# The skipped general path of two expert stages, moved ahead of the last scatter

## The reference

```python
def hier_moe(h, wg, bg, we, be, w_gate, w_up, w_down):
    t = h.reshape(-1, d)                                  # 256 tokens
    ...                                                   # top group of 4, then the best 2 of its 4 experts
    comb = ((g_oh * gw)[:, :, None] * w_grp[:, None, :]).reshape(n, MOE_EXPERTS)
    a = jax.nn.silu(jnp.einsum('td,edf->tef', t, w_gate)) * jnp.einsum('td,edf->tef', t, w_up)
    y = jnp.einsum('tef,efd->td', a * comb[:, :, None].astype(a.dtype), w_down)

x = x + g2 * hier_moe(h, ...)        # g2 is the gate; then comes the next layer's norm of x
```

## Time and profile before

| | us |
|---|---|
| median of 3 runs | 1435.12 |
| lowest and highest | 1433.93, 1435.15 |
| the profiled execution, its own time | 1437.19 |
| its span in the trace | 1435.4 |
| TensorE busy with matmuls | 1319.3 (92%) |
| VectorE busy | 446.6 (31%) |
| ScalarE busy | 237.7 (17%) |

### The profile page before, as it was taken

One profiled execution on the slowest core, in us unless ns is written; L12 is line 12 of the kernel. 1 busy time (PEld: TensorE's weight loads), 2 busy tenths in 40 slices (PEclk: granted clock), 3 DMA queues, 4 the chain that ended last, 5 costly groups with the idle time before them and its releaser, 6 DMA issues.

```text
span 1435.4 us, 18899 instructions
## 1 busy us (share of the span) xinstructions
PE 1319.3 (92%) x7788; PEld 682.9 (48%) x7788; DVE 446.6 (31%) x1251; ACT 237.7 (17%) x589; POOL 104.3 (7%) x196
## 2 busy tenths in 40 slices
PE   4999988999899899889998999989999699999996
PEld 3446644443545665444435864554545333333232
DVE  2004552221313574522215452351132711201113
ACT  0003310111101453101111221111320211010000
POOL 1100000000011000000001000000000021322111
PEclk8999999999999799999999999999999799999998
DMA  9957936999953664369998442364336579999990
GB/s 357 370 148 265 329 118 224 366 340 348 335 194 130 216 233 141 132 218 367 340 347 321 165 158 92 120 251 171 120 115 227 184 267 352 363 386 387 386 346 31
DMA packets 214763, 357.43 MB, mean 249 GB/s; under 512 B 15845, under 2 KB 86038, under 8 KB 214678
## 3 DMA queue, kind: packets, MB, share of 16 engines
q1 hardware_dynamic: 200864, 352.33, 69.1%
q10 hardware_dynamic: 13814, 3.87, 1.2%
HBM read 355.14 MB, written 1.05 MB: 248 GB/s over the span
## 4 chain that ended last, share of the span: by engine, by line
PE 83%; DVE 7%; DMA 4%; ACT 3%; issue 2%; SPq 0%; POOL 0%; DVEq 0%; ACTq 0%
PE bank L2055 19%; PE bank L2236 8%; PE bank L2433 7%; PE bank L2262 4%; PE bank L2277 4%; PE bank L2294 4%; PE bank L2723 4%; PE bank L2148 4%; PE bank L2507 3%; PE bank L2073 3%; PE bank L2772 3%; DMA ring<-in_w_down 3%; PE bank L2400 2%; PE bank L2542 2%; PE bank L2140 1%
## 5 line engine op out<-in xcount | busy, mean ns | idle before, releaser
L2055 PE MATMUL bank<-ring,hT 128*128 128x512 f32 x416 | 182.3, 597 | 2.6 <-ACT hT L878 2.4
L2055 PEld LDWEIGHTS bank<-ring,hT 128*128 128x128 f32 x416 | 78.7, 192 | 97.6 <-issue 97.6
L2236 PE MATMUL bank<-ring,A 128*64 128x512 f32 x512 | 113.4, 595 | 6.2 <-issue 3.2
L2055 PE MATMUL bank<-ring,OT 128*128 128x512 f32 x224 | 97.2, 593 | 1.3 <-ACT OT L1167 0.8
L2073 PE MATMUL bank<-ring,cact 128*32 128x128 f32 x2304 | 80.8, 295 | 13.7 <-DMA ring<-in_ada_w 7.5
L2433 PE MATMUL bank<-ring,A 128*64 128x512 f32 x384 | 86.8, 597 | 0.0
L746 POOL TENSOR_TENSOR rstd<-rstd,nhalf 128x1 f32<-128x1 f32 x20 | 17.2, 860 | 896.5 <-DVE rstd L1233 896.5
L2073 PEld LDWEIGHTS bank<-ring,cact 128*32 128x32 f32 x2304 | 67.8, 119 | 29.1 <-issue 21.5
L2262 PE MATMUL bank<-pb 128*128 128x128 f32 (+1 forms) x512 | 64.4, 279 | 7.7 <-DVE A L1451 5.4
L2236 PEld LDWEIGHTS bank<-ring,A 128*64 128x64 f32 x512 | 36.2, 137 | 72.0 <-issue 68.7
L2262 PEld LDWEIGHTS bank<-pb 128*128 128x128 f32 x512 | 59.6, 192 | 20.1 <-issue 11.4
(11 more groups left out here) (439 smaller groups left out, 1611.8 us busy)
## 6 DMA issues: line engine op xcount, KB each, us to landing
ring<-in_ada_w SPq DMA_DIRECT2D x24, 2048.0 KB, 9.3
ring<-in_moe_w_gate SPq DMA_DIRECT2D x32, 1024.0 KB, 8.0
ring<-in_moe_w_up SPq DMA_DIRECT2D x32, 1024.0 KB, 10.5
ring<-in_moe_w_down SPq DMA_DIRECT2D x16, 2048.0 KB, 12.8
ring<-in_w_gate SPq DMA_DIRECT2D x16, 2048.0 KB, 10.3
ring<-in_w_up SPq DMA_DIRECT2D x16, 2048.0 KB, 10.8
ring<-in_w_down SPq DMA_DIRECT2D x16, 2048.0 KB, 19.9
ring<-in_w_in SPq DMA_DIRECT2D x13, 2048.0 KB, 12.8
```

The lines of the kernel that those rows point to most:

```text
L2055: ins = mm(B[2 * (m % 2) + tt][:], lhs[:, c, tt * P:(tt + 1) * P], w[:, c, :], start=c == 0, stop=c == C - 1)
L2236: ins = mm(B[4][n * b:n * (b + 1), :], h3[:, c, n * b:n * (b + 1)], wv[b][:, :, c, :], start=c == 0, stop=c == C - 1)
```

## The change

In the first two expert stages the branch around the general path comes before the last scatter on TensorE, and before the wait for the summed banks on VectorE. So that a body that does run can add into the same banks, it no longer opens and closes them: `start` and `stop` follow `large`, which is true in "moe2" alone. Its spread weights go to B[4] to B[7], for which two waits are added inside the body, and VectorE's adds at the end of the body are left to the adds of the main path. The memset that counts `moe_added` stands behind those adds. In "moe2" the place is the same, and only the memset is gone.

```diff
@@ ScalarE, moe_rest_act
-                    a.copy(combT[:, 2 * j:2 * j + 2, :], B[j % 4][:]).then_inc(s[f"rest_act{i}"], 1)
+                    a.copy(combT[:, 2 * j:2 * j + 2, :],
+                           B[j % 4 if name == "moe2" else 4 + j % 4][:]).then_inc(s[f"rest_act{i}"], 1)
@@ VectorE, experts
             weighted(U - 1, 1)
+            moe_rest_dve(name, gate)
             dve.wait_ge(s["gate_rows"], 2 * i + 2)
             for tt in range(TT):
                 dve.wait_ge(s["moe_summed"], 2 * i + tt + 1)
...
             step(ins)
-            moe_rest_dve(name, gate)
+            v.memset(mark[:, 3:4], 0.0).then_inc(s["moe_added"], 1)
@@ VectorE, moe_rest_dve
-                dve.wait_ge(s[f"rest_used{i}"], 18)
-                for tt in range(TT):
...
-                dve.wait_ge(s[f"rest_step{i}"], masked + 8)
-            v.memset(mark[:, 3:4], 0.0).then_inc(s["moe_added"], 1)
+                if large:
+                    dve.wait_ge(s[f"rest_used{i}"], 18)
+                    for tt in range(TT):
...
+                    dve.wait_ge(s[f"rest_step{i}"], masked + 8)
@@ TensorE, experts
             weights(U - 1, 1)
+            moe_rest_pe(name)
             scatter(U - 1, 1, last=True)
-            moe_rest_pe(name)
@@ TensorE, moe_rest_pe
                 pe.wait_ge(s[f"rest_hid{i}"], 1)
+                if not large:
+                    units = MOE[name]["unit"] + MOE[name]["U"]
+                    pe.wait_ge(s["ye_out"], 2 * units)
+                    pe.wait_ge(s["swT_out"], units)
...
-                            ins = mm(B[j % 4][:, a * T + tt * P:a * T + (tt + 1) * P],
+                            ins = mm(B[j % 4 if large else 4 + j % 4][:, a * T + tt * P:a * T + (tt + 1) * P],
...
-                    ins = mm(B[b][:], zeros[:], bc(ident[:], 1, [P, 4, P]), start=True, stop=False)
+                    ins = mm(B[b][:], zeros[:], bc(ident[:], 1, [P, 4, P]), start=large, stop=False)
...
-                    ins = mm(B[b][:], zeros[:], bc(ident[:], 1, [P, 4, P]), start=False, stop=True)
+                    ins = mm(B[b][:], zeros[:], bc(ident[:], 1, [P, 4, P]), start=False, stop=large)
```

More of the change, by code:

```diff
@@ L1536, in moe_rest_dve @@
                     ins.then_inc(s[f"rest_hid{i}"], 1)
-                dve.wait_ge(s[f"rest_used{i}"], 18)
-                for tt in range(TT):
[L1539 to L1544, removed]
-                dve.wait_ge(s[f"rest_step{i}"], masked + 8)
-            v.memset(mark[:, 3:4], 0.0).then_inc(s["moe_added"], 1)
+                if large:
+                    dve.wait_ge(s[f"rest_used{i}"], 18)
+                    for tt in range(TT):
+                        for h in range(2):
+                            v.tensor_tensor(tmp[:, h, :], B[2 * tt + h][:], gate[:, 512 * h:512 * (h + 1)],
+                                            ALU.mult).then_inc(s[f"rest_step{i}"], 1)
+                            dve.wait_ge(s[f"rest_step{i}"], masked + 4 * tt + 2 * h + 1)
+                            xs = x[:, tt, 512 * h:512 * (h + 1)]
+                            v.tensor_tensor(xs, xs, tmp[:, h, :], ALU.add).then_inc(s[f"rest_step{i}"], 1)
+                    dve.wait_ge(s[f"rest_step{i}"], masked + 8)
         cs_flat = cs[:].rearrange("p a b -> p (a b)")
```

## The result

Ten executions of each kernel, on one chip: the changed kernel takes 1429.57 us (median, 1426.33 to 1432.15), the kernel before 1436.49 us (1433.93 to 1441.12). The ratio is 0.9949, with a 95% interval from 0.9937 to 0.9961, so the change makes it 0.5% faster, about 7 us. The profiled execution has a span of 1427.8 us, 7.6 less than before. The three runs of before that the prediction started from were low ones; with more, the median is 1436.5 to 1437.4.

A forecast was written before the change was run, and what follows sets the result against it. TensorE, busy 1319.3 of 1435.4 us, was taken to bound the kernel, with VectorE the chain after "moe1". Gains of 2.2 us after "moe0" and 0.9 after "moe1" made 3.1: 1435.1 to 1432.0 us, range 1430.9 to 1434.5.

The forecast's parts named there:

- The stop is a late block of code: TensorE's modulation group after "moe0": the 2.95 us stop is code fetched only after the jump over the long body.
- Moving the branch costs TensorE nothing: Ahead of the last scatter: the wait for `swT` gives 4.7 us of cover; without it, 1.3 us, twice.
- if the last scatter started later than 364.6: Sign of being wrong, after "moe0": the last scatter was to start no later than 364.6 us.
- After "moe0" VectorE is late next, at 2.27 us: Without the stop, VectorE's norm sets the modulation columns, at 377.75 instead of 380.02: 2.27 us, taken as 2.2.
- The price of the stop: After "moe0": without the stop TensorE's turn is done 2.95 us earlier; VectorE then decides, so 2.2 us is gained.
- At most the whole 2.95 us is gained: Upper bound after "moe0": the whole stop is gained if VectorE's norm is quicker than in the profiled execution.
- After "moe1", 0.9 us: VectorE is the chain there; its memset goes from 768.32 to 767.41, 0.91 us; TensorE's stop goes for nothing.
- The starting point: Whole kernel: the median of the runs before, 1435.12 us, from which 3.1 us was subtracted.
- (a): Rival, both stage ends: the stop shrinks only in part, 1.3 + 0.9 = 2.2 us, 1432.9; chance 0.2.
- (b): Rival: the stop is not code, or goes with the modulation group; 0.9 us are left, 1434.2; chance 0.12.
- (c): Rival: fetched code ends in the last scatter, the stop precedes the last sums; +2.9 us, 1438.0; chance 0.06.
- (d): Rival: the gain is taken up in a later wait for DMA, no change, 1435.1; chance 0.07.

The follow-up runs named there:

- the run with the short body: Kernel before, branch at its old place, TensorE's general path (not run here) left out in the first two expert stages: 1432.22 us, ratio 0.9983 to the kernel before.
- The idle time put in by hand: Changed kernel, but after "moe0" TensorE waits for VectorE's adds before the modulation group: 1439.72 us, ratio 1.0019 to the kernel before.

## Why the prediction was wrong

- **The stop is a late block of code**: right. It goes with the long body (the run with the short body), not with the branch or the group, and the packet comes 3.4 us behind the branch wherever that stands.
- **Moving the branch costs TensorE nothing**: right. The scatter starts 0.52 us behind the start of ScalarE's copy as before, and the branch is over 4.8 us earlier. One sign of being wrong was "if the last scatter started later than 364.6", and it started at 364.99; but the copy ahead of it came 0.40 us later too, so the shift comes from ahead of the stage's end, and the sign should have been tied to the copy.
- **After "moe0" VectorE is late next, at 2.27 us**: right for the profile at hand, where the columns moved 2.3 us against the scatter, as 380.02 - 364.59 = 15.43 became 378.10 - 364.99 = 13.11; to the start of the projection it made 2.65, since the transposes of that profile had a stop of 0.82 us of their own.
- **The price of the stop**: wrong, and this is the step that failed. The turn was to be done "2.95 us earlier", so the stop was counted at its own length, and the bounds said "At most the whole 2.95 us is gained". I took the stretch behind it, at full clock in the earlier trace rows, as what it always is. In six of seven profiles it ran at a lower clock instead. The term had 2.2 us and measured 4.0 (19.34 - 15.31). The idle time put in by hand shows that idle time alone is enough for the clock to fall, in the one execution that was profiled. That the first profile of before had full clock after "moe0" was chance; after "moe1" it showed the low one, 8.67 us for 250 matmuls, and I priced nothing by it.
- **After "moe1", 0.9 us**: right in mechanism, 0.7 in size (19.75 - 19.07). TensorE's transposes behind the longer idle time run slower (16 in 3.68 us, 0.23 us each, where in "moe0" of the changed kernel 8 take 1.06, 0.13 each). In the first profile of before, the first 8 of these had taken 1.20 and the other 8 1.94.
- **The starting point**: three runs with a median of 1435.12 stood for a kernel whose executions go from 1431 to 1441. The gain is not touched by it, the predicted time is by 1.4 to 2.3 us. The low start hid a part of the miss: from the later medians a gain of 3.1 us would have given 1433.4 to 1434.3.
- **The rivals**: (a), the stop only in part, did not occur; (b) to (d) are excluded by the rows above: the stop went with the branch, it stood in no other place, and the time fell. What I lacked was a rival in which the stop costs more than it lasts.

The stage ends make 4.0 + 0.7 = 4.7 us of the 6.5 to 6.9 measured. The clock near 597 us adds 0.7, by the change or by chance. The last 1 to 1.5 us stay open. The spans of the profiles, seven of before and five of the changed order, differ by 5.9 us in the mean, and scatter by 1.8 and 1.6 us (standard deviation) within each, so that a difference of 1 us between such means is within the noise and no place can be named for it.

## What to carry to other kernels

When TensorE stops for some 3 us amid work, take more than one profile before you price it, and read the time per matmul behind every such stop in the one you have. The stretch behind a stop can run in part at half the clock; here a stop of 3.01 us cost 20.70 - 15.31 = 5.4 at worst. A skipped branch over long code belongs ahead of a wait, if there is one that covers it (here 4.8 us), not behind it. And a part that stops saving when another engine becomes late is best priced together with that engine's own part: here 2.9 and nothing alone, 4.0 together.

## What was not expected of the hardware

- The sequencer of TensorE takes a branch over the long body in 0.33 to 0.38 us and only then, 5 to 17 matmuls on, comes to a stop; in the first profile it goes on 6.0 us behind the branch's end, while the weight loads keep the DMA at 387 GB/s. With the body of "moe2" the branch itself takes 3.34 us. Over a body of one wait it takes 0.23 us, and there is no stop.
- Behind 2.7 to 3.0 us without matmuls after "moe0" TensorE's granted clock fell in seven of nine profiles, and behind 3.97 us it did in the one profile; in the first profile of before, the engine was busy with matmuls throughout the 3.6 us ahead of the stop and at full level.
